# Multiplying only the used blocks in the merge levels of a chunk inverse (hybrid decoder layer, one core)

## The chip, the cores and the metric

The kernel runs on one core of a Trainium2 chip. The metric is the device time of one execution in microseconds (us), taken as the median of three runs. Lower is better.

## What is computed

The reference is one step of a one-layer hybrid decoder: a short convolution group and a gated delta network (GDN) group of 4 heads side by side, then a feed-forward layer. All of it is float32. This change touches one place only, the triangular solve inside a chunk of the GDN:

```python
lower = jnp.where(strict, jnp.einsum('nbhid,nbhjd->nbhij', kb, kc) * decay, 0.0)
eye = jnp.eye(chunk, dtype=jnp.float32)
...
sol = lax.linalg.triangular_solve(eye + lower, rhs, left_side=True, lower=True)
```

The kernel works with chunks ("tiles") of 128 tokens, so for each of the 8 prompt tiles t = 1 to 8 and each of the 4 heads it needs the inverse of a 128x128 unit lower triangular matrix.

## The kernel before

Everything is placed by hand in one instruction stream for each engine, with semaphores between them.

**Stages.** First the input projection (`w_in`, 28 weight tiles n, each multiplied in three column groups g, so the projection runs in units u = 3n + g). Then the output projection, the up projection and the down projection. A projection product is written as three float32r products (high x high, low x high, high x low: `dense_part`, L1699 to L1701). TensorE goes through these without a break. The GDN's small products are laid between the units by an order written out by hand: from unit u = 42 on, `round_step(u)` gives the tile t and a step s from 1 to 5, and `round_part(t, s)` issues that step right behind the dense part of its unit, on TensorE and on VectorE alike.

**The inverse.** The 32x32 blocks on the diagonal are inverted earlier. They are loaded as `X` (the inverse so far) and `Y` (its transpose), [128, 4 x 128], heads side by side. `At` is the transpose of the lower matrix. Two merge levels, k = 5 (blocks of 32 to 64) and k = 6 (64 to 128), each do: `level_p` multiplies `At` with `X` (L1919), VectorE's `keep_p` writes the product into `pairs{k}` (`pb[k]`) times a 0/1 mask that keeps only the blocks wanted (L2694), `level_xy` multiplies that with `Y` in both orders (level 5: L1932 and L1933, level 6: only L1933), and `keep_xy` subtracts the results from `X` (L2702, level 5 only) and `Y` (L2704). All results go through one PSUM bank, `L_BANK`.

**The steps of a round** for tile t, with a = t - 1, on TensorE: s = 1 `use_state(a)` (L1950, L1954), then `level_p(t, 5)`; s = 2 `next_state(a)` (L1964, L1967), then `level_xy(t, 5)`; s = 3 `level_p(t, 6)`, then `turn_k` (transposes, L1885); s = 4 `turn_o(a)` (transposes, L1977), `level_xy(t, 6)`, then `products_qk` (L1879); s = 5 `state_of_k` (L1902, it waits for level 6's `xy_kept`) and `turn_v`. Between two steps lies one unit of dense work. In the first round (t = 1) there is no tile a before it in this form. There `sample_states` (L2042, products with 48 rows) stands in front of each of the four steps.

**How a matmul shows.** A plain float32 matmul leaves two records on TensorE (and two weight loads). So the 4 heads of one level product are 8 records. A float32r product leaves one. A form such as `48*128 48x512` is read: 48 rows of the array (the contraction) by 128 columns (the stationary operand's), and a moving operand of 48 partitions x 512 elements.

**Masks and zeros.** The masks for the levels are a constant table, loaded to `c_levels` (`cg`, L730) by SyncE's queue. GpSimd zeroes `pairs5` and `pairs6` once (L1011, semaphore `pb_zero`), since `keep_p` writes only half of the columns. `pairs6` as zeros also feeds the DMAs that clear scratch memory (L734 to L737).

Of the kernel before, what the change touches and what calls it, by code (L numbers as in the profile page):

```python
# [7 lines left out]
ALU = mybir.AluOpType  # L8
# [5 lines left out]
P = 128  # L14
# [3 lines left out]
NH = 4  # L18
# [18 lines left out]
LEVELS = (5, 6)  # L37

# [39 lines left out]
NG = NH * (NT - 1)  # L78


def constants():
# [15 lines left out]
    g = []  # L97
    for k in LEVELS:
        b = 2 ** k
        first = np.arange(P // 2) // b  # L100
        r = np.arange(P)
        g.append(((r[:, None] // (2 * b) == first[None, :]) & (r[:, None] % (2 * b) >= b)).astype(np.float32))
# [4 lines left out]
    g.append(ahead)  # L107
    return main, np.concatenate(g, axis=1).astype(np.float32)


def build(nc, x_prompt, x_sample, state_conv_a, state_conv_qkv, state_ssm, meta_tokens, norm_mix, w_in,
# [4 lines left out]
    with ctx:  # L116
# [120 lines left out]
        cg = place("c_levels", [P, P], F32, FREE + 7 * HB)  # L237
        ahead_big = place("ahead_big", [P, P], F32, FREE + 7 * HB + 512)
        assert FREE + 7 * HB + 1024 <= R1
        lev = {k: cg[:, P // 2 * i:P // 2 * (i + 1)] for i, k in enumerate(LEVELS)}  # L240

# [124 lines left out]
        s_levels = sem("s_levels"); s_ahead = sem("s_ahead"); s_states = sem("s_states")  # L366
# [226 lines left out]
        def first(ap, b):  # L593

            return ap.rearrange("p (n two b) -> p n two b", two=2, b=b)[:, :, 0, :]

        def second(ap, b):
            return ap.rearrange("p (n two b) -> p n two b", two=2, b=b)[:, :, 1, :]

        def per_head(ap, c, w):  # L600

            return ap.unsqueeze(2).to_broadcast([c, NH, w])

# [51 lines left out]
        def _(sp):  # L655
# [69 lines left out]
            def step(u):  # L725
                n, g = u // 3, u % 3
                if g == 0 and n == 1:
                    sp.wait_ge(x_turned, 3 * KT)
                    sp.dma_start(g_picks[:, :], c_main[0:2 * NG, 2 * P + 2 * C0 + 2 * NH:]).then_inc(s_ahead, 16)
                    sp.dma_start(cg[:, :], c_gdn[:, 0:P]).then_inc(s_levels, 16)  # L730
                    sp.dma_start(ahead_big[:, :], c_gdn[:, P:2 * P]).then_inc(s_ahead, 16)
                    sp.dma_start(ahead_small[:, :], c_gdn[:, 2 * P:2 * P + C0]).then_inc(s_ahead, 16)
                    sp.wait_ge(pb_zero, 2)
# [209 lines left out]
        def _(pool):  # L943
# [62 lines left out]
            def zero_pairs():  # L1006

                pool.wait_ge(ab_made, 3)
                pool.wait_ge(rows_kept, 3)
                for k in LEVELS:  # L1010
                    pool.memset(pb[k][:, :], 0.0).then_inc(pb_zero, 1)  # L1011
# [680 lines left out]
        def _(pe):  # L1692
# [212 lines left out]
            def level_p(t, k):  # L1905
# [11 lines left out]
                for h in range(NH):  # L1917
                    hs = slice(P * h, P * h + P)
                    ins = pe.matmul(ps[L_BANK][:, hs], At[:, hs], X[:, hs], start=True, stop=True)  # L1919
                ins.then_inc(p_made, 1)  # L1920

            def level_xy(t, k):
# [6 lines left out]
                for h in range(NH):  # L1929
                    hs = slice(P * h, P * h + P)  # L1930
                    if not last:
                        pe.matmul(ps[L_BANK][:, hs], Y[t % 2][:, hs], pb[k][:, hs], start=True, stop=False)  # L1932
                    ins = pe.matmul(ps[L_BANK][:, hs], pb[k][:, hs], Y[t % 2][:, hs], start=last, stop=True)  # L1933
# [399 lines left out]
        def _(dve):  # L2333
# [351 lines left out]
            def keep_p(t, k):  # L2685
                m, b = len(LEVELS) * (t - 1) + LEVELS.index(k), 2 ** k
                dve.wait_ge(p_made, m + 1)
                if t == 1:
                    dve.wait_ge(s_levels, 16)
                    dve.wait_ge(zeroed, 16 * (2 * NT - 1))  # L2690
                src = ps[L_BANK][:, :].rearrange("p (h n two b) -> p h n two b", h=NH, two=2, b=b)[:, :, :, 0, :]
                dst = pb[k][:, :].rearrange("p (h n two b) -> p h n two b", h=NH, two=2, b=b)[:, :, :, 0, :]
                mask = lev[k].rearrange("p (n b) -> p n b", b=b).unsqueeze(1).to_broadcast([P, NH, P // 2 // b, b])
                dve.tensor_tensor(dst, src, mask, ALU.mult).then_inc(p_kept, 1)  # L2694
# [614 lines left out]
```

## Time and profile before

| | us |
|---|---|
| median of 3 runs | 1294.07 (1293.22 to 1294.09) |
| the profiled execution's own time | 1292.4 |
| its span in the profile | 1290.6 |
| TensorE matmul busy in the span | 1271.4 (99%) |
| VectorE busy | 811.9 (63%) |
| GpSimd busy | 658.5 (51%) |
| ScalarE busy | 462.2 (36%) |

The span is the time between the first and the last instruction that the profiler recorded. The profiled execution is 1.8 us longer than its span, and 1.7 us under the median. Busy times of matmuls are modelled and overlap each other, so the price of a matmul in a stream is read from the distance between the starts of two records, not from how long one record is. The granted TensorE clock is 0.997 of full speed over the span.

### The profile page before, as it was taken

The page shows a single profiled execution, that of the slowest core. Times are in us where ns is not written, and L with a number is a line of the kernel's source. Part 1 is how long each engine was busy: PE and PEld are TensorE (multiplying, and loading weights), DVE is VectorE, ACT ScalarE, POOL GpSimd, SP SyncE. Part 2 cuts the span into 40 slices and gives each one's busy share as a digit, 9 for nine tenths or more (in the row PEclk, how much of TensorE's full clock was granted, in tenths as well). Part 3 has the DMA queues.
Part 4 walks back from the last instruction along what each step waited for, and adds up shares of the span by engine and source line. Part 5 has one row for each costly group of instructions (what it writes and reads, how often), then busy time and mean ns, then how long its engine had stood idle before and what let it go on. Part 6 is the DMA issues. An engine that isn't in the chain of part 4 may idle for free.

```text
span 1290.6 us, 23252 instructions
## 1 busy us (share of the span) xinstructions
PE 1271.4 (99%) x9392; PEld 1240.8 (96%) x9392; DVE 811.9 (63%) x1252; ACT 462.2 (36%) x769; POOL 658.5 (51%) x501
## 2 busy tenths in 40 slices
PE   7999999999999999999999999999999999999997
PEld 6899999899999999999989999999999999999997
DVE  6566799434555647655887775656567767557446
ACT  7566562122212212323423233332444533333303
POOL 1322112111212111212689988888879989788701
PEclk9999999999999999999999999999999999999999
DMA  6222561743332222222134434434655343542002
GB/s 199 59 80 79 161 193 52 189 134 95 88 82 68 80 74 76 86 80 67 34 135 174 150 143 150 155 121 167 219 188 201 140 160 102 181 137 85 17 18 118
DMA packets 164860, 152.91 MB, mean 118 GB/s; under 512 B 21111, under 2 KB 141459, under 8 KB 162066
## 3 DMA queue, kind: packets, MB, share of 16 engines
q1 hardware_dynamic: 141778, 138.55, 33.3%
q10 hardware_dynamic: 22976, 12.88, 3.7%
q8 instruction: 75, 1.23, 0.4%
q14 instruction: 31, 0.25, 0.1%
HBM read 104.11 MB, written 47.29 MB: 117 GB/s over the span
## 4 chain that ended last, share of the span: by engine, by line
PE 89%; DVE 4%; issue 3%; ACT 1%; POOL 1%; DMA 1%; SPq 0%; POOLq 0%; DVEq 0%; ACTq 0%
PE banks L2224 15%; PE banks L2227 15%; PE banks L2226 15%; PE banks L1699 10%; PE banks L1701 10%; PE banks L1700 10%; PE banks L2271 1%; PE banks L2272 1%; PE banks L2273 1%; PE banks L1919 1%; PE banks L1933 1%; PE banks L2155 1%; DMA w_raw<-in_w_in 1%; DVE hT L3119 1%; PE banks L2279 1%
## 5 line engine op out<-in xcount | busy, mean ns | idle before, releaser
L1699 PE MATMUL banks<-xn_high,w_high 128*128 128x384 f32 (+1 forms) x672 | 227.5, 338 | 1.2 <-DVE xn_low L2369 1.2
L1701 PE MATMUL banks<-xn_high,w_low 128*128 128x384 f32 (+1 forms) x672 | 218.7, 325 | 0.0
L1700 PE MATMUL banks<-xn_low,w_high 128*128 128x384 f32 (+1 forms) x672 | 218.5, 325 | 0.0
L959 POOL TENSOR_TENSOR w_low<-w_raw,w_high 128x1024 fp32r<-128x1024 f32 x30 | 75.0, 2500 | 232.8 <-ACT w_high L1219 232.8
L2224 PE MATMUL banks<-op_high,set_high 128*128 128x264 f32 x672 | 191.3, 285 | 0.2
L2227 PE MATMUL banks<-op_high,set_low 128*128 128x264 f32 x672 | 190.8, 284 | 0.0
L2226 PE MATMUL banks<-op_low,set_high 128*128 128x264 f32 x672 | 190.5, 283 | 0.0
L3119 DVE TENSOR_TENSOR hT<-hT,banks 128x528 f32<-128x528 f32 x148 | 100.7, 700 | 106.6 <-PE banks L2227 106.2
L1102 POOL TENSOR_TENSOR set_low<-w_up_raw,set_high 128x512 fp32r<-128x512 f32 x79 | 122.7, 1553 | 60.2 <-ACT set_high L1528 60.2
L2224 PE MATMUL banks<-up_high_T,set_high 128*128 128x264 f32 x496 | 141.6, 285 | 0.9 <-POOL up_low_T L1109 0.6
L2227 PE MATMUL banks<-up_high_T,set_low 128*128 128x264 f32 x496 | 140.8, 284 | 0.0
L2226 PE MATMUL banks<-up_low_T,set_high 128*128 128x264 f32 x496 | 140.6, 283 | 0.0
L1699 PEld LDWEIGHTS banks<-xn_high,w_high 128*128 128x128 f32 x672 | 126.9, 189 | 3.9 <-DVE w_low L2363 1.2
L1700 PEld LDWEIGHTS banks<-xn_low,w_high 128*128 128x128 f32 x672 | 127.3, 189 | 0.0
L2224 PEld LDWEIGHTS banks<-op_high,set_high 128*128 128x128 f32 x672 | 126.3, 188 | 0.6 <-DVE op_low L3129 0.3
L1701 PEld LDWEIGHTS banks<-xn_high,w_low 128*128 128x128 f32 x672 | 126.7, 189 | 0.0
L2227 PEld LDWEIGHTS banks<-op_high,set_low 128*128 128x128 f32 x672 | 126.4, 188 | 0.0
L2226 PEld LDWEIGHTS banks<-op_low,set_high 128*128 128x128 f32 x672 | 126.3, 188 | 0.0
L2224 PE MATMUL banks<-up_high_B,set_high 128*128 128x264 f32 x408 | 116.5, 286 | 1.9 <-DVE u_rows L3028 1.6
L2227 PE MATMUL banks<-up_high_B,set_low 128*128 128x264 f32 x408 | 115.9, 284 | 0.0
L2226 PE MATMUL banks<-up_low_B,set_high 128*128 128x264 f32 x408 | 115.7, 284 | 0.0
L2224 PEld LDWEIGHTS banks<-up_high_T,set_high 128*128 128x128 f32 x496 | 93.2, 188 | 1.5 <-POOL up_low_T L1109 0.8
(383 smaller groups left out, 3141.7 us busy)
## 6 DMA issues: line engine op xcount, KB each, us to landing
op_raw<-ops_kept SPq DMA_DIRECT2D x21, 1056.0 KB, 5.0
w_up_raw<-in_w_up SPq DMA_DIRECT2D x16, 1024.0 KB, 5.5
ops_kept<-u_rows SPq DMA_DIRECT2D x28, 528.0 KB, 2.8
w_raw<-in_w_in SPq DMA_DIRECT2D x28, 512.0 KB, 4.1
ops_kept<-u_T SPq DMA_DIRECT2D x42, 264.0 KB, 2.0
w_down_half<-in_w_down SPq DMA_DIRECT2D x3, 2048.0 KB, 8.3
w_down<-in_w_down SPq DMA_DIRECT2D x24, 256.0 KB, 4.0
w_raw<-in_w_out SPq DMA_DIRECT2D x8, 512.0 KB, 4.0
```

The costliest lines, as they stand in the source:

```text
L959: pool.tensor_tensor(w_l[n % 2][:, :, :], w_raw[n % 2][:, :, :], w_h[n % 2][:, :, :].bitcast(F32), ALU.subtract).then_inc(w_low, 1)
L1102: pool.tensor_tensor(set_l[s % 4][:, :, :], up_source_at(s), set_h[s % 4][:, :, :].bitcast(F32), ALU.subtract).then_inc(w_low, 1)
L1699: pe.matmul(bank[:, 0:w], w_h[n % 2][:, k, :], hi[:, c0:c0 + w], start=(k == first), stop=False)
L1700: pe.matmul(bank[:, 0:w], w_h[n % 2][:, k, :], lo[:, c0:c0 + w], start=False, stop=False)
L1701: ins = pe.matmul(bank[:, 0:w], w_l[n % 2][:, k, :], hi[:, c0:c0 + w], start=False, stop=(k == last))
L1919: ins = pe.matmul(ps[L_BANK][:, hs], At[:, hs], X[:, hs], start=True, stop=True)
L1933: ins = pe.matmul(ps[L_BANK][:, hs], pb[k][:, hs], Y[t % 2][:, hs], start=last, stop=True)
L2155: ins = pe.transpose(ps[6 + m % 2][:, o:o + c], (xs0, xs)[f % 2][0:c, t, :], eye[0:c, 0:c])
L2224: pe.matmul(bank, high[:, j, :], op_high[:, j, cols], start=(j == 0 and not begun), stop=False, skip_group_check=True)
L2226: pe.matmul(bank, high[:, j, :], op_low[:, j, cols], start=False, stop=False, skip_group_check=True)
L2227: ins = pe.matmul(bank, low[:, j, :], op_high[:, j, cols], start=False, stop=(j == n - 1), skip_group_check=True)
L3119: dve.tensor_tensor(hc, hc, both, ALU.add if sign > 0 else ALU.subtract).then_inc(acc_read_dve, 1)
```

## The change

Both levels multiply only the blocks that the merge uses, as separate small matmuls, each on the part of TensorE's array that the partitions of its operands and its result select. `corner(ap, n, rows_at, cols_at)` is a 32x32 block per head of pair n (n = 0, 1) of 64 rows.

- Level 5, `level_p`: instead of one 128x128 product a head, two of 32 x 32 x 32 (n = 0 and 1). `level_xy`: instead of two 128x128 products a head, four of 32 x 32 x 32.
- Level 6, `level_p` and `level_xy`: instead of one 128x128 product a head, one of 64 x 64 x 64.
- `keep_p`: instead of one multiply with the mask (128 partitions x 256 elements), plain copies: at level 5 two of 32 partitions x 128 elements, at level 6 one of 64 partitions x 256 elements.
- `keep_xy`: at level 5 four subtractions of 32 partitions x 128 elements instead of two of 128 x 256; at level 6 one of 64 partitions x 256 elements instead of one of 128 x 256.
- The mask table, its DMA and semaphore `s_levels`, and the zeroing of `pairs5` go.

```diff
@@ constants and loads
-        cg = place("c_levels", [P, P], F32, FREE + 7 * HB)
...
-                    sp.dma_start(cg[:, :], c_gdn[:, 0:P]).then_inc(s_levels, 16)
...
-                    sp.wait_ge(pb_zero, 2)
+                    sp.wait_ge(pb_zero, 1)
...
-                for k in LEVELS:
-                    pool.memset(pb[k][:, :], 0.0).then_inc(pb_zero, 1)
+                pool.memset(pb[LEVELS[-1]][:, :], 0.0).then_inc(pb_zero, 1)
...
+        def corner(ap, n, rows_at, cols_at):
+
+            return h3(ap)[2 * B * n + rows_at:2 * B * n + rows_at + B, :, 2 * B * n + cols_at:2 * B * n + cols_at + B]
@@ level_p
-                    hs = slice(P * h, P * h + P)
-                    ins = pe.matmul(ps[L_BANK][:, hs], At[:, hs], X[:, hs], start=True, stop=True)
+                    if k == LEVELS[-1]:
+                        up, low = slice(P * h, P * h + W), slice(P * h + W, P * h + P)
+                        ins = pe.matmul(ps[L_BANK][W:P, up], At[0:W, low], X[0:W, up], start=True, stop=True)
+                    else:
+                        for n in range(2):
+                            ins = pe.matmul(corner(ps[L_BANK], n, B, 0)[:, h, :], corner(At[:, :], n, 0, B)[:, h, :],
+                                            corner(X[:, :], n, 0, 0)[:, h, :], start=True, stop=True)
@@ level_xy
-                    if not last:
-                        pe.matmul(ps[L_BANK][:, hs], Y[t % 2][:, hs], pb[k][:, hs], start=True, stop=False)
-                    ins = pe.matmul(ps[L_BANK][:, hs], pb[k][:, hs], Y[t % 2][:, hs], start=last, stop=True)
+                    if last:
+                        up, low = slice(P * h, P * h + W), slice(P * h + W, P * h + P)
+                        ins = pe.matmul(ps[L_BANK][0:W, low], pb[k][W:P, up], Y[t % 2][W:P, low], start=True, stop=True)
+                    else:
+                        for n in range(2):
+                            made = corner(pb[k][:, :], n, B, 0)[:, h, :]
+                            turned = corner(Y[t % 2][:, :], n, B, B)[:, h, :]
+                            pe.matmul(corner(ps[L_BANK], n, B, 0)[:, h, :], turned, made, start=True, stop=True)
+                            ins = pe.matmul(corner(ps[L_BANK], n, 0, B)[:, h, :], made, turned, start=True, stop=True)
@@ keep_p
-                dve.tensor_tensor(dst, src, mask, ALU.mult).then_inc(p_kept, 1)
+                if k == LEVELS[-1]:
+                    ins = dve.tensor_copy(h3(pb[k][W:P, :])[:, :, 0:W], h3(ps[L_BANK][W:P, :])[:, :, 0:W])
+                else:
+                    if t == 1:
+                        dve.wait_ge(zeroed, 16 * (2 * NT - 1))
+                    for n in range(2):
+                        ins = dve.tensor_copy(corner(pb[k][:, :], n, B, 0), corner(ps[L_BANK], n, B, 0))
+                ins.then_inc(p_kept, 1)
@@ keep_xy
-                ys = second(Y[t % 2][:, :], b)
-                dve.tensor_tensor(ys, ys, second(made, b), ALU.subtract).then_inc(xy_kept, 1)
+                if k == LEVELS[-1]:
+                    ys = h3(Y[t % 2][0:W, :])[:, :, W:P]
+                    ins = dve.tensor_tensor(ys, ys, h3(ps[L_BANK][0:W, :])[:, :, W:P], ALU.subtract)
+                else:
+                    for n in range(2):
+                        xs_, ys = corner(X[:, :], n, B, 0), corner(Y[t % 2][:, :], n, 0, B)
+                        dve.tensor_tensor(xs_, xs_, corner(ps[L_BANK], n, B, 0), ALU.subtract)
+                        ins = dve.tensor_tensor(ys, ys, corner(ps[L_BANK], n, 0, B), ALU.subtract)
+                ins.then_inc(xy_kept, 1)
```

Here `P` is 128, `W` is 64 and `B` is 32.

## Rows read from the trace of the kernel before

**Rows 1.** The page: busy times, and the chain that ended last.

```profile
PE 1271.4 (99%) x9392; PEld 1240.8 (96%) x9392; DVE 811.9 (63%) x1252; ACT 462.2 (36%) x769; POOL 658.5 (51%) x501
...
PE 89%; DVE 4%; issue 3%; ACT 1%; POOL 1%; DMA 1%; SPq 0%; POOLq 0%; DVEq 0%; ACTq 0%
```

**Rows 2.** All waits of TensorE, 240 to 500 us: total, times, longest.

```profile
PE banks L1977 <- DVE o_tok L2746: 0.2, 1, 0.2
```

**Rows 3.** Groups by line, TensorE, 240 to 500 us: busy us, mean ns.

```profile
L1933 PE MATMUL banks<-Y,pairs 128*128 128x128 f32 x128 | 20.9, 276 | 0.0
L1919 PE MATMUL banks<-X,At 128*128 128x128 f32 x128 | 17.1, 276 | 0.0
L1932 PE MATMUL banks<-pairs,Y 128*128 128x128 f32 x64 | 12.5, 277 | 0.0
```

**Rows 4.** Timeline, TensorE, steps 1 and 2 of round 2: start, us, what.

```profile
281.97 1.06 PE L1919 MATMUL banks<-X,At 128*128 128x128 f32 x8
282.79 0.39 PE L1699 MATMUL banks<-xn_high,w_high 128*128 128x304 f32 x1
...
288.00 0.39 PE L1932 MATMUL banks<-pairs,Y 128*128 128x128 f32 x2
...
289.56 0.39 PE L1933 MATMUL banks<-Y,pairs 128*128 128x128 f32 x2
289.71 0.42 PE L1699 MATMUL banks<-xn_high,w_high 128*128 128x384 f32 x1
289.97 0.34 PE L1700 MATMUL banks<-xn_low,w_high 128*128 128x384 f32 x1
```

**Rows 5.** Timeline, TensorE, steps 3 and 4 of round 2.

```profile
293.98 1.05 PE L1919 MATMUL banks<-X,At 128*128 128x128 f32 x8
294.87 0.60 PE L1885 MATMUL banks<-c_main,k_feat 128*128 128x128 f32 x4
...
299.94 1.06 PE L1933 MATMUL banks<-Y,pairs 128*128 128x128 f32 x8
300.83 0.61 PE L1879 MATMUL banks<-q_feat,k_feat 128*128 128x128 f32 x4
```

**Rows 6.** Timeline, TensorE, 245.5 to 246.2 us, step 1 of round 1.

```profile
245.02 1.02 PE L2042 MATMUL banks<-v_masked,kd_t 48*128 48x512 f32 x2
245.97 0.49 PE L1919 MATMUL banks<-X,At 128*128 128x128 f32 x2
```

**Rows 7.** Timeline, TensorE, around 178.8 us: window up to 178.86, then 179.9.

```profile
178.57 0.27 PE L1885 MATMUL banks<-c_main,k_feat 128*48 128x128 f32 x1
178.78 0.29 PE L1879 MATMUL banks<-q_feat,k_feat 128*48 128x48 f32 x2
...
178.78 0.56 PE L1879 MATMUL banks<-q_feat,k_feat 128*48 128x48 f32 x8
179.26 0.44 PE L1699 MATMUL banks<-xn_high,w_high 128*128 128x384 f32 x1
179.54 0.33 PE L1700 MATMUL banks<-xn_low,w_high 128*128 128x384 f32 x1
```

**Rows 8.** Timeline, TensorE, around 200 us: window up to 199.92, then 201.2.

```profile
199.75 0.42 PE L1891 MATMUL banks<-Y_t,kg 48*128 48x48 f32 x2
...
199.75 1.09 PE L1891 MATMUL banks<-Y_t,kg 48*128 48x48 f32 x8
200.77 0.41 PE L1699 MATMUL banks<-xn_high,w_high 128*128 128x304 f32 x1
```

**Rows 9.** Timeline, VectorE, 277 to 291 us.

```profile
277.42 1.13 DVE L2674 SCALAR_TENSOR_TENSOR vn<-banks,egn,vn 128x128 f32<-128x128 f32 x4 [2.40 <-ACT vn L1397]
...
283.07 0.42 DVE L2694 TENSOR_TENSOR pairs<-banks,c_levels 128x256 f32<-128x256 f32 x1 [0.20 <-PE banks L1919]
...
290.33 0.41 DVE L2704 TENSOR_TENSOR Y<-Y,banks 128x256 f32<-128x256 f32 x1
```

**Rows 10.** Windows: us, busy us of PE, PEld, DVE, ACT, POOL, granted clock, DMA share, GB/s.

```profile
238.60:242.00 3.40, 3.40 (x15) 2.97 (x14) 2.41 (x3) 1.65 (x8) 0.00 (x0) 0.51 0.16 53
```

More of the change, by code:

```diff
@@ L37 @@
 LEVELS = (5, 6)
+B = SOLVED
 IN_TILES = ([("k", h, O_QKV + NH * P + P * h) for h in range(NH)] + [("q", h, O_QKV + P * h) for h in range(NH)]
@@ L78 @@
 NG = NH * (NT - 1)
+W = P // 2
 def constants():
@@ L96, in constants @@
     main[:2 * NG, o + 2 * NH + NT - 1:] = row % NH == np.arange(NH)[None, :]
-    g = []
-    for k in LEVELS:
[L99 to L102, printed above, removed]
     ahead = np.zeros((P, P + C0), np.float32)
@@ L106, in constants @@
     ahead[:C0, P:] = np.where(same & up[:C0, :C0], 0, FAR_BELOW)
-    g.append(ahead)
-    return main, np.concatenate(g, axis=1).astype(np.float32)
+    return main, ahead
 def build(nc, x_prompt, x_sample, state_conv_a, state_conv_qkv, state_ssm, meta_tokens, norm_mix, w_in,
@@ L236, in build @@
         kd = place("kd", [P, NH * P], F32, FREE + 6 * HB)
-        cg = place("c_levels", [P, P], F32, FREE + 7 * HB)
-        ahead_big = place("ahead_big", [P, P], F32, FREE + 7 * HB + 512)
-        assert FREE + 7 * HB + 1024 <= R1
-        lev = {k: cg[:, P // 2 * i:P // 2 * (i + 1)] for i, k in enumerate(LEVELS)}
+        ahead_big = place("ahead_big", [P, P], F32, FREE + 7 * HB)
+        assert FREE + 7 * HB + 512 <= R1
         SB = SOLVED * SOLVED
@@ L591, in h3 @@
             return ap.rearrange("p (h i) -> p h i", h=NH)
[L593 to L598, printed above, removed]
         def per_head(ap, c, w):
             return ap.unsqueeze(2).to_broadcast([c, NH, w])
+        def corner(ap, n, rows_at, cols_at):
+            return h3(ap)[2 * B * n + rows_at:2 * B * n + rows_at + B, :, 2 * B * n + cols_at:2 * B * n + cols_at + B]
         def hrow(f):
@@ L1009, in zero_pairs @@
                 pool.wait_ge(rows_kept, 3)
-                for k in LEVELS:
-                    pool.memset(pb[k][:, :], 0.0).then_inc(pb_zero, 1)
+                pool.memset(pb[LEVELS[-1]][:, :], 0.0).then_inc(pb_zero, 1)
             def identities():
@@ L2685, in keep_p @@
             def keep_p(t, k):
-                m, b = len(LEVELS) * (t - 1) + LEVELS.index(k), 2 ** k
+                m = len(LEVELS) * (t - 1) + LEVELS.index(k)
                 dve.wait_ge(p_made, m + 1)
[L2688 to L2693, printed above, removed]
-                dve.tensor_tensor(dst, src, mask, ALU.mult).then_inc(p_kept, 1)
+                if k == LEVELS[-1]:
[6 more added lines that the diff above has]
+                ins.then_inc(p_kept, 1)
             def keep_xy(t, k):
-                m, b = len(LEVELS) * (t - 1) + LEVELS.index(k), 2 ** k
+                m = len(LEVELS) * (t - 1) + LEVELS.index(k)
                 dve.wait_ge(xy_made, m + 1)
-                made = ps[L_BANK][:, :]
-                if k != LEVELS[-1]:
-                    xf = first(X[:, :], b)
-                    dve.tensor_tensor(xf, xf, first(made, b), ALU.subtract)
-                ys = second(Y[t % 2][:, :], b)
-                dve.tensor_tensor(ys, ys, second(made, b), ALU.subtract).then_inc(xy_kept, 1)
+                if k == LEVELS[-1]:
[7 more added lines that the diff above has]
+                ins.then_inc(xy_kept, 1)
             def keep_v(t):
```

7 lines of the change are left out of this document (3 added, 4 removed).

## The prediction

> **What bounds the kernel.** I read the page first, for who is busy and who is last: TensorE's matmuls fill 99% of the span and 89% of the chain that ended last [rows 1]. Then the waits, to see whether TensorE ever stands for something else in the stretch that changes: in 240 to 500 us it waits 0.2 us in all [rows 2]. So whatever TensorE saves there shortens the kernel, and whatever it pays there lengthens it. The work that the change touches is 128 + 64 + 128 = 320 records [rows 3]. Their mean of 276 ns is a pipelined length, not a price. The price is the pitch between starts: the timeline of one round has 8 records between 293.98 and 294.87 and again between 299.94 and 300.83 [rows 5], 0.112 us each. All 320 cost 35.7 us of TensorE.
>
> **Prices for small blocks.** No row shows a 32x32 or 64x64 block, so I take them from the narrowest forms, and read four numbers from two groups of 8 records. I write m for the columns of the stationary operand and n for those of the moving one.
>
> - Pitch in the stream: with m = n = 48, records 3 to 8 add 0.56 - 0.29 = 0.27 us, or 0.045 each [rows 7]. With m = 128, n = 48 they add 1.09 - 0.42 = 0.67, or 0.112 [rows 8], the same as 128x128. So the larger of m and n sets it, and a line through both is 0.005 us + 0.00084 per column: 0.0315 at 32, 0.0585 at 64.
> - Entering: the first narrow record starts 178.78 - 178.57 = 0.21 us behind the last full one [rows 7] where 0.11 is usual, so going from the whole array to a part costs about 0.09.
> - The second record of a group is not overlapped: its distance is a group of two less the length of its last record (0.208 for 48x48, 0.27 for the others): 0.29 - 0.21 = 0.08 at 48x48 [rows 7], 0.42 - 0.27 = 0.15 at 128 and 48 [rows 8], 0.49 - 0.28 = 0.21 at 128 and 128 [rows 6]. That is load and multiply one behind the other, 0.053 at 32 and 0.107 at 64.
> - Leaving: the last narrow record starts at 178.78 + 0.56 - 0.21 = 179.13, the dense work at 179.26, 0.13 to 0.14 later; from the group with m = 128 it is 200.77 - (199.75 + 1.09 - 0.27) = 0.20 [rows 8]. So leaving is the pitch plus 0.09: 0.12 at 32, 0.15 at 64. The dense record after that follows at 0.28 [rows 7], where it is 0.26 in an ordinary exit [rows 4].
>
> **TensorE, step by step, t = 2 to 8.** Each stretch runs from the last untouched record before the level product to the second one after it.
>
> - Step 1: before, 0.11 in, 8 x 0.112 to the dense work less the overlap of its start, which is 282.79 - 281.97 = 0.82 [rows 4], then 0.26: 0.11 + 0.82 + 0.26 = 1.19. After, 16 records: 0.20 + 0.053 + 14 x 0.0315 + 0.12 + 0.28 = 1.09. Saved 0.10.
> - Step 2: before, 0.11 + (289.97 - 288.00) = 2.08 [rows 4]. After, 32 records: 0.20 + 0.053 + 30 x 0.0315 + 0.12 + 0.28 = 1.60. Saved 0.48.
> - Step 3: before, 0.17 in, 0.89 for the records [rows 5], 0.11 to the second transpose: 1.17. After, 8 records at 64: 0.27 + 0.107 + 6 x 0.0585 + 0.15 + 0.14 (the usual 0.11 and some of the lost overlap) = 1.02. Saved 0.15.
> - Step 4: before, 0.11 + 0.89 [rows 5] + 0.11 = 1.11. After: 0.20 + 0.107 + 0.351 + 0.15 + 0.21 (two full loads in a row, [rows 6]) = 1.02. Saved 0.09.
>
> That is 0.82 us a tile, 5.7 us for seven. In the first round the level products stand behind `sample_states`, which uses 48 rows: the kernel before pays there already, 0.52 where 0.43 is usual and 0.21 where 0.11 is [rows 6]. So entering is 0.19 cheaper in each of the four steps, and the tile saves 0.82 + 0.76 = 1.6 us. Sum: 7.3 us. Note how little level 6 and step 1 bring: about 60% of the arithmetic's saving is given back at the eight changes between whole array and part in each round. Step 2 alone carries 60% of the gain, and only if 32-wide records really come every 0.03 us.
>
> **VectorE and the waits.** At level 5 `keep_p` becomes two operations of 128 elements for one of 256, `keep_xy` four for two. A 128-element operation that reads PSUM costs 1.13 / 4 = 0.28 us, one with 256 costs 0.41 to 0.42 [rows 9]. So VectorE pays 6 x 0.28 - 3 x 0.42 = +0.44 us a tile, 3.5 us in all. Level 6 keeps its 256 elements a partition, and I cost it at nothing. None of this is on the path: the level 5 product is kept at 283.5 [rows 9] and used at 288.00 [rows 4], `keep_xy` ends at 290.7 [rows 9] and step 3 needs it at 293.98 [rows 5]. The cover is 3.2 us against +0.3 us. Queued behind `keep_xy` in step 3 is `keep_k`, whose reader is two dense units away. If the cover were gone, the cost would be that 0.3 us a tile, 2.4 us. The mask's DMA (SyncE's queue, with two small loads behind it) and one memset of GpSimd go at 41 to 47 us, where TensorE waits for neither queue: nothing.
>
> **Sum.** Against the profiled execution: span 1290.6 - 7.3 = 1283.3, its time 1292.4 - 7.3 = 1285.1. The median of the runs lies 1.7 above that execution, so 1294.07 - 7.3 = 1286.8 us.
>
> **Rivals.**
>
> - *Parts run side by side: faster still.* At level 5 neighbouring matmuls alternate between parts of the array (n = 0 and 1; in step 2 also two column parts): 7 changes of part in step 1 and 15 in step 2. If each change cost only 0.005 us of a pitch, it would save 0.027 x 22 = 0.6 us a tile, 4.8 in all: 1282.0. Against it: the pitch at m = 128, n = 48 is set by the weight load [rows 8], and loads would have to overlap too. The Trainium skill (TensorEngine Tiling (Array Packing), Key Properties) says that they do: different tiles execute weight loads and matmuls in parallel. No row of this trace has two parts at work, so it can't agree or disagree; by that rule the time is this rival's. Chance 0.15.
> - *Small records don't come faster than 0.045 us.* The narrowest stream here is 0.045 [rows 7], and a floor of issue could sit just there. Then level 5 costs 48 x 0.0135 = 0.65 us a tile more, 5.2 in all: a gain of 2.1, 1292.0, no change. Between that row and the line's 0.0315 I take the line, since rows 7 and 8 show the price following the columns. Chance 0.13.
> - *A change of part drains the array: slower.* Going from whole to part costs 0.09 and the lost overlap of the next record 0.02. If going from one part to another of the same size costs the same, 0.11, then if only changes of row part count, 14 a tile x 0.11 = 1.5 us, 12 us in all and 1299; if all 22 count, 19 us and 1306. It decides at 0.91 / 22 = 0.04 us a change, which is 0.065 with 14. The Trainium skill (TensorEngine Tiling (Array Packing), Gotcha 1) speaks for it: different row tiles cannot access the same PSUM bank simultaneously, and all these results go to one bank. Its Key Properties speak against it, for they name a drain only where the mode changes, not the tile. If only the overlap of load and multiply is lost at a change (0.0215 each), the gain is 3.5 us, still faster. Chance of slower 0.13.
> - *The clock falls.* Behind a long row of 48-wide products the granted clock was 0.51 for 3.4 us [rows 10], some 1.7 us lost. That is the lower level, 1.2 GHz. Once behind each step 2, it would cost 13.6 us: 1300. Against: each level stretch here is 1.0 to 1.6 us, with dense work before and behind. Chance 0.04.
> - *Something that TensorE didn't wait for is late* (VectorE's extra time, a weight tile): 1292, chance 0.03.
>
> **Chances and range.** The forecast, a gain between 3.5 (overlap lost at each change) and 9.8 (0.025 us a record at level 5), 1284.3 to 1290.6, has 0.52. About 0.2% (2.6 us) is what a measurement of this kernel tells from no change. Faster: 0.52 + 0.15 and a third of the floor rival, as a floor of 0.04 still gives 4 us: 0.71. Same: 0.12. Slower: 0.13 + 0.04: 0.17. The range reaches down to the overlap rival and up past the floor rival, leaving out the drain and the clock: 1281.0 to 1294.5.
>
> **What the changed profile would show.** 512 records in place of 320. Step 1's 16 records from first to last start in 0.50 us and step 2's 32 in 1.0 if the pitch is right; 0.7 and 1.4 with the floor; about 1.3 and 1.8 with a drain at changes of row part. Each level group entered 0.20 us behind the record before, left by its pitch plus 0.09. In the first round no extra at the entry. TensorE's waits in 240 to 490 us still near zero and clock 1.00. VectorE with 24 more operations (8 a tile for 5) and 3.5 us more. I am wrong if the pitch at level 5 isn't 0.03, if entering from a transposing matmul to 64 columns costs more than the 0.09 seen at 48, or if the time saved comes back as TensorE waits in the projections behind.

## The result, and the profile after

The changed kernel takes 1280.13 us (median of 4 runs, 1279.20 to 1281.01), the kernel before 1293.64 us on the same chip (1291.47 to 1294.09). The ratio is 0.9896 (95% interval 0.9884 to 0.9908): 13.5 us faster. The forecast was 1286.8, with a range whose lower end was 1281.0. The sign was right and the gain 6.2 us too small. The remaining 0.4 us is the lower median of the kernel before in this comparison. The profiled execution took 1279.97 us, its span is 1278.2.

The page of the kernel after, busy times and then the chain that ended last, beside [rows 1]:

```profile
PE 1257.5 (98%) x9584; PEld 1221.3 (96%) x9584; DVE 821.8 (64%) x1276; ACT 462.4 (36%) x769; POOL 656.3 (51%) x500
...
PE 90%; DVE 5%; issue 3%; ACT 1%; DMA 1%; SPq 0%; POOLq 0%; POOL 0%; DVEq 0%; ACTq 0%
```

TensorE is still the bound. It has 192 records more, and 14 us less of busy time. Groups by line and form, TensorE, 240 to 500 us of the kernel after, to be read beside [rows 3] (busy us, mean ns of one):

```profile
L1908 PE MATMUL banks<-X,At 64*64 64x64 f32 x64 | 5.4, 224 | 0.0
L1925 PE MATMUL banks<-Y,pairs 64*64 64x64 f32 x64 | 5.4, 224 | 0.0
L1931 PE MATMUL banks<-Y,pairs 32*32 32x32 f32 x128 | 3.6, 194 | 0.0
L1930 PE MATMUL banks<-pairs,Y 32*32 32x32 f32 x128 | 3.6, 194 | 0.0
L1911 PE MATMUL banks<-X,At 32*32 32x32 f32 x128 | 3.5, 194 | 0.0
```

All 320 records of [rows 3] have become 512. The mean of one fell only from 276 to 194 ns, and again it is not the price. At level 5 a record is 194 ns long, yet 128 of them fill 3.5 us of busy time, 0.027 us each. Busy time here is the union of overlapping records, and so many are in flight at once.

Timeline of the kernel after, TensorE, step 1 of round 2, then the first records and the exit of step 2 (start, us, what), beside [rows 4]:

```profile
279.64 0.44 PE L1911 MATMUL banks<-X,At 32*32 32x32 f32 x16
280.01 0.41 PE L1687 MATMUL banks<-xn_high,w_high 128*128 128x304 f32 x1
...
285.34 0.21 PE L1930 MATMUL banks<-pairs,Y 32*32 32x32 f32 x1
285.35 0.21 PE L1931 MATMUL banks<-Y,pairs 32*32 32x32 f32 x1
285.35 0.21 PE L1930 MATMUL banks<-pairs,Y 32*32 32x32 f32 x1
285.36 0.21 PE L1931 MATMUL banks<-Y,pairs 32*32 32x32 f32 x1
285.39 0.19 PE L1930 MATMUL banks<-pairs,Y 32*32 32x32 f32 x1
...
285.60 0.19 PE L1931 MATMUL banks<-Y,pairs 32*32 32x32 f32 x1
285.72 0.45 PE L1687 MATMUL banks<-xn_high,w_high 128*128 128x384 f32 x1
```

Step 1's group of 16 starts at 279.64 and ends at 280.08; less the 0.19 of its last record, its records start within 0.25 us. I had predicted 0.50. In step 2 the 32 records start between 285.34 and 285.60, in 0.26 us, where I had predicted 1.0. The four parts (n = 0 and 1, each with a product of either order) start 6 or 7 ns apart. The next record of the same part comes some 0.03 us behind the last (0.05 for a part's second record). So the price that I put on every record, 0.0315, is the price of a record on its own part, and four parts pay it at the same time. Step 2 has four times the arithmetic of one part and takes no longer than step 1, which uses two.

Steps 3 and 4 of the same round, beside [rows 5]:

```profile
289.84 0.34 PE L1689 MATMUL banks<-xn_high,w_low 128*128 128x384 f32 x1
290.11 0.67 PE L1908 MATMUL banks<-X,At 64*64 64x64 f32 x8
290.71 0.55 PE L1873 MATMUL banks<-c_main,k_feat 128*128 128x128 f32 x3
...
295.73 0.27 PE L1975 MATMUL banks<-c_main,o_tok 128*128 128x128 f32 x1
295.93 0.68 PE L1925 MATMUL banks<-Y,pairs 64*64 64x64 f32 x8
296.54 0.49 PE L1867 MATMUL banks<-q_feat,k_feat 128*128 128x128 f32 x2
```

Here everything is as priced: entered 0.27 behind a dense record and 0.20 behind a transpose, and 0.60 and 0.61 us from the first narrow record to the work behind (0.107 + 6 x 0.0585 + 0.15 = 0.61). The 64x64 products all use one part.

The waits of TensorE, 240 to 500 us (total, times, longest), beside [rows 2]:

```profile
PE banks L1975 <- DVE o_tok L2748: 0.7, 2, 0.4
PE banks L1687 <- DVE ya_low L2577: 0.5, 1, 0.5
```

1.2 us in place of 0.2, but only the first line is new. The wait for `ya_low` is there in the kernel before too, just behind the window of [rows 2]:

```profile
507.45 0.40 PE L1699 MATMUL banks<-ya_high,w_high 128*128 128x288 f32 x1 [0.48 <-DVE ya_low L2579]
```

With everything some 14 us earlier, it has moved into the window. So the waits for `o_tok` rose from 0.2 to 0.7 us, and that is all. On VectorE the level's operations in the same window are these (busy us, mean ns):

```profile
L2692 DVE COPY pairs<-banks 32x128 f32<-32x128 f32 x16 | 4.6, 290 | 0.4
L2704 DVE TENSOR_TENSOR X<-X,banks 32x128 f32<-32x128 f32 x16 | 4.6, 287 | 0.4
L2705 DVE TENSOR_TENSOR Y<-Y,banks 32x128 f32<-32x128 f32 x16 | 4.5, 280 | 0.2
L2687 DVE COPY pairs<-banks 64x256 f32<-64x256 f32 x8 | 3.4, 427 | 4.7 <-PE banks L1908 4.5
L2700 DVE TENSOR_TENSOR Y<-Y,banks 64x256 f32<-64x256 f32 x8 | 3.2, 401 | 0.0
```

That is 20.3 us. Before, the level's operations took 16.6 there, so VectorE does 3.7 us more (3.5 predicted).

**Where the 13.5 us come from.** I aligned the two traces on the same dense records. Between 211 us of the kernel before and 518 us, the end of the last round, the kernel after gains 16.0 us. Of this 15.2 are the levels: that much shorter are the stretches of the four steps (from the last untouched record to the second one behind), added up over the eight tiles, 13.0 at level 5 and 2.2 at level 6. It is also what the 7.3 of my sum and 0.98 us a tile x 8 = 7.9 at level 5 make together. Another 1.5 is the clock fall of [rows 10], which this execution doesn't show. About 0.7 goes back to the waits for `o_tok`: there the transposes start 0.72 and 0.58 us behind the record before them, in rounds 3 and 4, where the kernel before has 0.18 and 0.45. The span is only 12.4 shorter, though. 1.65 us are lost at the start, where the full clock was first granted at 17.7 us instead of 13.4, and 1.9 us behind this line of VectorE's timeline in the kernel after:

```profile
636.09 8.27 DVE L3081 SCALAR_TENSOR_TENSOR u_rows<-u_rows,h_squares 128x1056 f32<-128x1056 f32 x1
644.28 0.69 DVE L3052 TENSOR_TENSOR u_rows<-u_rows,banks 128x528 f32<-128x528 f32 x1
```

The same operation took 2.06 us in the kernel before. TensorE waited 3.2 us for its successor (1.6 in the kernel before), and the granted clock fell behind the wait for 3.4 us. The first experiment asks whether that belongs to the change.

### The profile page after: what moved, and what is told of

Read it like the earlier page. It is cut to its first block, busy times and chain, and to the rows that moved or that the text cites. A ratio compares the mean times of both kernels' runs of the same rounds, so it can differ in the third digit from the quotient of the medians.

```text
span 1278.2 us, 23657 instructions
## 1 busy us (share of the span) xinstructions
PE 1257.5 (98%) x9584; PEld 1221.3 (96%) x9584; DVE 821.8 (64%) x1276; ACT 462.4 (36%) x769; POOL 656.3 (51%) x500
## 4 chain that ended last, share of the span: by engine, by line
PE 90%; DVE 5%; issue 3%; ACT 1%; DMA 1%; SPq 0%; POOLq 0%; POOL 0%; DVEq 0%; ACTq 0%
PE banks L2222 15%; PE banks L2225 15%; PE banks L2224 15%; PE banks L1687 10%; PE banks L1689 10%; PE banks L1688 10%; PE banks L2269 1%; PE banks L2270 1%; PE banks L2271 1%; PE banks L2153 1%; PE banks L1867 1%; DMA w_raw<-in_w_in 1%; DVE hT L3121 1%; PE banks L2277 1%; PE banks L2040 1%
```

## The experiments

Theories. **A**: parts of the array run side by side, so a level 5 step costs what its busiest part costs. **B**: the small records are simply cheaper than I thought, one behind another, each some 0.016 us in step 1 and 0.008 in step 2. Other candidates are VectorE's new form, the missing mask and its DMA, and chance events outside the rounds. The expectations of by_part and level6_columns use the letters A and B for pairs of their own, which they spell out.

| kernel | median us (range, runs) | before us | ratio (95%) |
|---|---|---|---|
| copy | 1279.35 (1278.89 to 1282.68, 6) | 1293.29 | 0.9905 (0.9890 to 0.9920) |
| level6_only | 1291.28 (1289.56 to 1293.68, 12) | 1293.29 | 0.9986 (0.9977 to 0.9996) |
| level5_only | 1283.44 (1280.72 to 1283.62, 6) | 1293.29 | 0.9923 (0.9910 to 0.9936) |
| by_part | 1282.74 (1281.44 to 1287.40, 6) | 1293.29 | 0.9930 (0.9912 to 0.9948) |
| one_pair | 1280.31 (1278.04 to 1281.16, 4) | 1293.83 | 0.9895 (0.9880 to 0.9910) |
| twice | 1284.45 (1282.20 to 1285.44, 5) | 1293.83 | 0.9921 (0.9908 to 0.9933) |
| vector_only | 1293.25 (1291.56 to 1295.77, 11) | 1293.83 | 0.9995 (0.9987 to 1.0004) |
| same_size_together | 1277.14 (1274.95 to 1277.87, 4) | 1293.83 | 0.9866 (0.9852 to 0.9879) |
| by_two | 1278.88 (1277.03 to 1281.71, 5) | 1295.43 | 0.9888 (0.9869 to 0.9907) |
| level6_columns | 1276.35 (1274.19 to 1277.39, 4) | 1295.43 | 0.9861 (0.9838 to 0.9884) |

**copy.** The changed kernel once more, with no edit.

> The changed kernel once more. If its time is its own, about 1280 us again, 13.5 under the kernel before. In its profile: the level 5 records again 6 ns apart on different parts, 16 records of step 1 from first to last start in 0.25 us and 32 of step 2 in 0.26. Open is whether three things of its first profile come again: full clock granted 4.3 us later at the start (1.65 us lost), one VectorE operation of 8.3 us at 636 us (normally 1.2), and the fall of the clock behind TensorE's wait for it at 645 us. If they are chance, they are gone or elsewhere.

1279.35 us. In its profile the same operation of VectorE is ordinary, and there is no clock fall at 645 us:

```profile
636.74 2.07 DVE L3081 SCALAR_TENSOR_TENSOR u_rows<-u_rows,h_squares 128x1056 f32<-128x1056 f32 x1
```

So the 8.27 us were an event of one execution. GpSimd's timelines beside it, first in the kernel after, then in the copy, show what went with it:

```profile
636.99 1.29 POOL L1090 TENSOR_TENSOR set_low<-w_up_raw,set_high 128x512 fp32r<-128x512 f32 x1
...
641.98 1.26 POOL L1090 TENSOR_TENSOR set_low<-w_up_raw,set_high 128x512 fp32r<-128x512 f32 x1
```

```profile
637.61 2.35 POOL L1090 TENSOR_TENSOR set_low<-w_up_raw,set_high 128x512 fp32r<-128x512 f32 x1
```

In the kernel after, GpSimd's operations follow each other without a gap up to 643.24, each 1.3 us long, and VectorE's operation ends only behind them, at 644.36. In the copy VectorE's operation is short, and GpSimd's, started during it, is the one that takes 1.1 us more. So one of the two engines stood while the other worked, and in the first profile it was VectorE, through five operations of GpSimd. That is read from these two profiles and was not tested.

From first to last start the levels' groups agree with those of the first profile to 0.01 us in every round. The ledger is now simpler: start of the kernel -2.1 us (full clock granted at 18.5 us), 211 to 518 us +15.8, everything behind 0. The waits for `o_tok` are there again, 0.8 us in all, so these do belong to the change. The longer one is in step 4 of round 3, where `turn_o` waits while VectorE still works through the convolution taps ahead of it (one of these takes 2.36 us at 319.05, where 0.23 is usual, beside an operation of GpSimd; the kernel before has such a stretch of 2.2 us in the same round):

```profile
325.19 0.55 PE L1975 MATMUL banks<-c_main,o_tok 128*128 128x128 f32 x3 [0.51 <-DVE o_tok L2748]
```

From round 2 to round 3 the level 5 product comes 1.78 us sooner than before (28.61 us apart instead of 30.39). My step prices with side by side parts give 0.82 + 0.98 = 1.80. The next round brings only 1.02. The wait of 0.5 us falls in it, and with the wait the overlap of the records around it is lost: the transposes start 0.85 us behind the record before them, where 0.18 is usual.

**level6_only and level5_only.** Each keeps one level's products as before (128x128) and has the other's as after. VectorE is as after in both. `level_xy` is edited like `level_p`, and level6_only zeroes `pairs5` as before, since its 128x128 products read all of it.

```diff
# level6_only, in level_p and level_xy, level 5
-                        for n in range(2):
-                            ins = pe.matmul(corner(ps[L_BANK], n, B, 0)[:, h, :], corner(At[:, :], n, 0, B)[:, h, :],
-                                            corner(X[:, :], n, 0, 0)[:, h, :], start=True, stop=True)
+                        hs = slice(P * h, P * h + P)
+                        ins = pe.matmul(ps[L_BANK][:, hs], At[:, hs], X[:, hs], start=True, stop=True)
# level5_only, level 6
-                        ins = pe.matmul(ps[L_BANK][W:P, up], At[0:W, low], X[0:W, up], start=True, stop=True)
+                        hs = slice(P * h, P * h + P)
+                        ins = pe.matmul(ps[L_BANK][:, hs], At[:, hs], X[:, hs], start=True, stop=True)
```

> Level 6's 64x64 products alone, level 5's matmuls 128x128 as before (its corners copied by VectorE, pairs5 zeroed again). Both theories price it at 0.24 us a tile plus 0.38 in the first round, 2.3 us: about 1291.3. If entering and leaving the 64x64 part cost more than the 0.09 us each that I took, it is no gain at all, 1293.6.

> Level 5 as in the changed kernel, level 6's matmuls again 128x128 (VectorE's operations as in the changed kernel). Theory, parts work side by side at level 5: level 6 is worth 0.24 us a tile and 0.38 more in the first round, 2.3 us, so this keeps 11.2 of the 13.5 us: about 1282.4. Rival, level 5's records come one behind the other as I priced them and the gain beyond the forecast is from elsewhere: 7.3 - 2.3 = 5.0 us under before, 1288.6.

level6_only gained 2.0 us (0.5 to 3.0), 2.2 by the stretches of its steps 3 and 4: the 64x64 prices were right. level5_only gained 9.9 us, with an interval of 8.3 to 11.6. With level 5 at my prices it would have gained about 5. So the surprise sits in level 5 alone. In the profile of level5_only the stretches of steps 1 and 2 are 13.0 us shorter than before, just as in the changed kernel. From 211 us to the end of the rounds it gains 12.3, the rest going to the waits for `o_tok`. Its start loses 1.95 us and a clock fall at 59 us another 1.55, so its span is 8.8 shorter. Losses of this kind are most likely why the medians give less than the stretches.

**by_part.** The level 5 products of one part stand together, and then those of the next part. Same records, other order.

```diff
-                for h in range(NH):
...
-                        for n in range(2):
+                    for n in range(2):
+                        for h in range(NH):
                             ins = pe.matmul(corner(ps[L_BANK], n, B, 0)[:, h, :], corner(At[:, :], n, 0, B)[:, h, :],
...
                             pe.matmul(corner(ps[L_BANK], n, B, 0)[:, h, :], turned, made, start=True, stop=True)
+                        for h in range(NH):
+                            made = corner(pb[k][:, :], n, B, 0)[:, h, :]
+                            turned = corner(Y[t % 2][:, :], n, B, B)[:, h, :]
                             ins = pe.matmul(corner(ps[L_BANK], n, 0, B)[:, h, :], made, turned, start=True, stop=True)
```

> Same matmuls as the changed kernel, but at level 5 all four heads of one part are issued before the next part begins, so that neighbours in the stream are on the same part. Theory A, parts only overlap when neighbours in the stream are on different parts: step 1 takes 0.50 us and step 2 1.0 again, 0.98 us a tile more, 7.9 in all: about 1288. Theory B, the engine looks past matmuls that wait for their part to later ones on a free part: no change, 1280, and the records of different parts stand 6 ns apart, out of the program's order.

Neither number came. The order does matter: step 1 took 0.40 us and step 2 0.70, where it was 0.25 and 0.26. That makes 0.59 us a tile and 4.7 us in all by the trace, and 3.4 by the medians, of runs that spread over 6 us; in part the later TensorE waits less for `o_tok` (0.3 us for 0.8). Theory B, in which a record's price doesn't depend on its neighbour, falls with this. But the parts still overlap in part. Timeline of by_part, step 2 of round 2:

```profile
289.41 0.34 PE L1932 MATMUL banks<-pairs,Y 32*32 32x32 f32 x5
289.56 0.21 PE L1936 MATMUL banks<-Y,pairs 32*32 32x32 f32 x1
289.59 0.19 PE L1932 MATMUL banks<-pairs,Y 32*32 32x32 f32 x1
...
289.98 0.32 PE L1936 MATMUL banks<-Y,pairs 32*32 32x32 f32 x5
290.23 0.45 PE L1687 MATMUL banks<-xn_high,w_high 128*128 128x384 f32 x1
```

Five records of the first part start alone; then a record of the second part starts right behind the fifth, and the two alternate. The second part's records stand behind all 8 of the first part's in the program. So the first part's sixth, seventh and eighth records were already out of the way when the second part's first one began, and it started ahead of them. The account that fits is a queue in front of each part. Records leave in program order, each part can hold three waiting records behind the one at work, and a fourth stops the stream for everybody. Starts of the four parts by that account: 0, 0.148, 0.306, 0.459, last record at 0.70. Measured: 0, 0.153, 0.306, 0.460 and 0.702. It was formed after this run and from it, so it needed another.

**by_two.** The four heads in two pairs, and inside each pair the order of by_part.

```diff
-                for h in range(NH):
...
-                        for n in range(2):
+                    for h2 in (0, 2):
+                      for n in range(2):
+                        for h in (h2, h2 + 1):
```

> As by_part, but only two heads (4 records) of one part stand together before the next part begins. In the trace of by_part the second part's first record started 6 ns behind the fifth of the first part's eight, so with three records still waiting between them. If the engine can pass over three waiting records, then here the second part begins at once and two parts are always at work: step 1 takes 0.25 to 0.28 us from first to last start (0.40 in by_part), step 2 about 0.50 (0.70 in by_part, 0.26 in the changed kernel), 0.26 us a tile more than the changed kernel, 2.1 us: about 1281.5. If it can't look ahead at all, step 1 takes 0.45 and step 2 0.9: 1286.

Step 1 took 0.269 us, as expected. Step 2 took 0.295 to 0.297, not 0.50. (This profile lists a granted clock of 0.95 up to 1150 us, but its rounds keep the copy's pace to 0.5%, 28.75 us from round 2 to 3 for 28.61, so the steps can be set beside the others.) Its first records are these:

```profile
286.77 0.21 PE L1934 MATMUL banks<-pairs,Y 32*32 32x32 f32 x1
286.79 0.21 PE L1938 MATMUL banks<-Y,pairs 32*32 32x32 f32 x1
286.80 0.21 PE L1934 MATMUL banks<-pairs,Y 32*32 32x32 f32 x1
286.81 0.21 PE L1938 MATMUL banks<-Y,pairs 32*32 32x32 f32 x1
```

All four parts are at work within 0.04 us, though the fourth part's first record stands behind 12 others in the program, 9 of which had not started. So a limit of three records for all parts together, on which I had built the 0.50, is wrong. With three waiting places for each part, no part of by_two ever has a fourth one in wait at the start, and the stream runs freely. That limit fits both kernels. It rests on the starts in these two, and a test made for it alone was not run. At 1278.88 us this kernel can't be told from the copy.

**one_pair.** It leaves out the second block pair (n = 1) of level 5, on TensorE and VectorE, so that half of level 5's products and of its operations on VectorE are not done.

```diff
-                        for n in range(2):
+                        for n in range(1):
```

> Leaves work out: at level 5 only the first pair of blocks (n = 0) is multiplied and kept, so half of level 5's matmuls and of its VectorE operations are gone and the lower half of the inverse isn't merged at this level. Theory, parts work side by side and a part takes 0.032 us a record: the first part's 8 records in step 1 and the 8 on each of two parts in step 2 still take 0.25 us each, so the time is that of the changed kernel, 1279.4 us within 0.5. Rival, the engine simply issues small records every 0.016 and 0.008 us whichever part they are on: step 1 and step 2 shrink to half, 0.25 us a tile, 2 us less: 1277.4.

The timeline of step 1, round 2, of one_pair, 8 records where the changed kernel has 16:

```profile
280.30 0.43 PE L1911 MATMUL banks<-X,At 32*32 32x32 f32 x8
280.67 0.41 PE L1687 MATMUL banks<-xn_high,w_high 128*128 128x304 f32 x1
```

0.37 us from the first record to the dense work, as with 16 records (279.64 to 280.01). First to last it is 0.243 for 0.249, and in step 2 0.250 for 0.263. Half of the multiplying left out saves TensorE 0.02 us a tile, and the time, 1280.31, is that of the changed kernel. This is the plainest evidence for theory A: the second row part is free.

**twice.** Each level 5 product is issued twice, into the same place.

```diff
-                        for n in range(2):
+                        for n in (0, 1, 0, 1):
```

> At level 5 each product is made twice over (same result), so every part has 16 records instead of 8 in both steps; neighbours in the stream are still on different parts. Theory: a part takes 0.032 us a record, so both steps go from 0.25 to 0.51 us between first and last start, 0.51 us a tile more, 4.1 us: about 1283.4. If the issue of records were the limit in step 2 (64 records, 0.006 apart would be 0.38), step 2 would stay under 0.51.

In step 1 of round 2 it is 0.62 us from the first record (282.31) to the dense work (282.93), 0.503 of them first to last; step 2's 64 records took 0.562. A step costs 8 records of its part more, 0.25 to 0.30. Step 2 went past the 0.51 that I expected: its first 32 records start within 0.263 us, as in the changed kernel, but the other 32 need 0.288, where 8 records of a part at 0.0315 make 0.25. So issue at 6 ns a record was not the limit, but with four parts and 64 records something slows the stream a little, and no run shows what. With eight tiles that is 4.4 us by the trace, and the medians differ by 5.1 (1284.45 and 1279.35, of two comparisons).

**vector_only.** The kernel before on TensorE, with VectorE's copies and corner subtractions, no masks and no mask DMA. `pairs5` is zeroed as before.

```diff
-                dve.tensor_tensor(dst, src, mask, ALU.mult).then_inc(p_kept, 1)
+                    for n in range(2):
+                        ins = dve.tensor_copy(corner(pb[k][:, :], n, B, 0), corner(ps[L_BANK], n, B, 0))
```

> TensorE's level products are the 128x128 ones of the kernel before, only VectorE's part of the change is in: unmasked copies of the corners, 64 operations for 40, 3.5 us more of VectorE by my working; pairs5 zeroed as before. It was costed at nothing: 1293.3 within 0.5. If VectorE's extra time were on the path somewhere, up to 3 us more: 1296.

A ratio of 0.9995: nothing, as priced. The masks, their load and 3.7 us of VectorE are worth nothing either way while TensorE comes no earlier.

**same_size_together.** The changed kernel, with the 48-row products of tile 0 regrouped (`use_state` and `next_state` of tile 0), so that matmuls of one form follow each other. Two small ones elsewhere are swapped for the same reason.

```diff
                 for h in range(NH):
-                    hs, cs = slice(P * h, P * h + P), slice(C0 * h, C0 * h + C0)
+                    hs = slice(P * h, P * h + P)
                     pe.matmul(ps[S_BANK][:, hs], kd0[:, hs], v_meta[:, hs], start=True, stop=True)
+                for h in range(NH):
+                    hs, cs = slice(P * h, P * h + P), slice(C0 * h, C0 * h + C0)
                     ins = pe.matmul(ps[O_BANK][0:C0, hs], qk0[:, cs], vnew[0:C0, hs], start=True, stop=True)
```

> The changed kernel, and in addition the products of tile 0 that alternate between 48 and 128 rows or columns are put together by size: in next_state0 four of L2029's kind and then four of L2030's, in use_state0 the same (only the first product of the bank opens with the flag that clears it), and two products of the decay sums are swapped. If every change of size costs 0.09 us and the lost overlap of the record behind it (0.035 to 0.10), 6 changes less in next_state0 save 1.0 us, 6 in use_state0 0.75, 2 in the sums 0.2: 1.9 us in all, 1277.4. If the price stems from the level products' own place only, nothing: 1279.4.

Timeline of the copy, first and last row of `next_state` of tile 0:

```profile
238.12 0.49 PE L2027 MATMUL banks<-v_meta,kd_t 48*128 48x128 f32 x2
...
240.82 0.42 PE L2028 MATMUL banks<-v_new,qk 48*48 48x128 f32 x2
241.16 0.41 PE L1687 MATMUL banks<-xn_high,w_high 128*128 128x304 f32 x1
```

The same in same_size_together:

```profile
236.52 1.16 PE L2031 MATMUL banks<-v_meta,kd_t 48*128 48x128 f32 x8
237.60 1.07 PE L2034 MATMUL banks<-v_new,qk 48*48 48x128 f32 x8
238.60 0.41 PE L1687 MATMUL banks<-xn_high,w_high 128*128 128x304 f32 x1
```

3.04 us became 2.08. In `use_state` of tile 0 it is 0.78 less. 12 changes between forms go, 6 in each, so one costs 0.13 to 0.16 us. Of these 1.7 us the profile gives 0.4 back in round 3, where the level 5 product starts 0.57 us behind the record before it instead of 0.21; the profile names no releaser. The kernel takes 1277.14 us, 2.2 less than the copy of another comparison; against the kernel before the two ratios are 0.9866 and 0.9905. I had expected 1.9.

**level6_columns.** same_size_together, with each 64x64 product of level 6 cut into two of 64 rows x 32 columns, on two column parts.

```diff
-                        ins = pe.matmul(ps[L_BANK][W:P, up], At[0:W, low], X[0:W, up], start=True, stop=True)
+                        for c in range(2):
+                            o = W + B * c
+                            ins = pe.matmul(ps[L_BANK][o:o + B, up], At[0:W, P * h + o:P * h + o + B], X[0:W, up],
+                                            start=True, stop=True)
```

> same_size_together, and in addition each 64x64x64 product of level 6 is made as two products with 32 columns of the stationary operand each (64 rows, moving operand 64 columns), on two column parts. Theory A, the larger of the stationary and the moving columns sets a part's pitch: 0.058 us a record still, both parts side by side, so 16 records take 0.46 us from first to last start as 8 did: 1277.1, no change. Theory B, the columns of the weight load set it: 0.032, 0.25 us instead of 0.46 in two steps, 3.3 us less: 1273.8.

```profile
288.43 0.64 PE L1910 MATMUL banks<-X,At 64*32 64x64 f32 x16
289.00 0.55 PE L1873 MATMUL banks<-c_main,k_feat 128*128 128x128 f32 x3
```

0.42 us from the first to the last of 16 records, against 0.457 for 8 undivided ones. The 64 moving columns still set the pitch (0.056), and halving the stationary columns saves mostly at a part's second record (0.080 for 0.107). The two steps save 0.07 us a tile, 0.56 in all; 1276.35 against 1277.14 is no difference that these runs can tell. It is still the fastest kernel of the study by its median, with same_size_together beside it.

## Why the prediction was wrong

**The step that failed** is the price of level 5's records in the stream. In steps 1 and 2 I wrote "14 x 0.0315" and "30 x 0.0315", one record behind another. The line through [rows 7, 8] was right for one part: in one_pair 8 records on one row part took 0.243 us, where 0.053 + 6 x 0.0315 gives 0.242. What was wrong is that the records add up over parts. Step 1 cost 0.25 instead of 0.49 and step 2 0.26 instead of 1.00: 0.98 us a tile, 7.9 in all. That is the whole miss of 6.2 us in the gain and 1.7 us more. The waits for `o_tok` give back 0.7 to 0.9 of it; the rest is within the interval of the comparison (1.5 us either way).

**The rival "parts run side by side"** was the right one, and I mis-sized it twice. It got 0.15, and its price was wrong. I let only the change from one part to the next be cheap ("only 0.005 us of a pitch"), so that a pair of records still cost 0.0365; that gave 4.8 us more. But records that run side by side are not a chain with cheap links. The cost is the longest part's own records, 8 in both steps, and so step 2 costs what step 1 costs. That form of the sentence gives 7.9 us, and 1278.9 as the time, before the new waits. The measured step times of 0.249 and 0.262 differ only by the 6 or 7 ns of the other parts' starts. The Trainium skill (TensorEngine Tiling (Array Packing), Key Properties) says that different tiles can execute weight loads and matmuls in parallel. The trace agrees, with four parts started 6 to 7 ns apart; one_pair shows that a second row part costs 0.02 us a tile, and twice that 8 more records on each part cost 0.25 to 0.30 us a step.

**The drain rival** is refuted: neighbouring records on different row parts, with results in the same PSUM bank, start 6 or 7 ns apart, where it wanted 0.11 us. It had leaned on the sentence of the Trainium skill (TensorEngine Tiling (Array Packing), Gotcha 1) that different row tiles cannot access the same PSUM bank simultaneously. Here products on two row parts (0 and 2 in step 1, 1 and 3 in step 2) write different partitions of one bank, and none waits for it; the measurement decides.

**The floor of 0.045** is refuted too: 0.032 on one part, 0.008 over four.

**What held.** Entering at 0.20 behind a full record (205 ns measured at 32, 202 and 268 at 64). The second record's 0.107 at 64. The pitch of 0.0585 at 64 (58 to 59 ns). Leaving at 0.12 and 0.15 (120 and 149 ns). No extra at the entry in the first round. Steps 3 and 4 as a whole, which level6_only shows by itself: 1291.28. VectorE's +3.5 us (3.7), off the path as long as TensorE keeps its old pace (vector_only). The mask and its DMA at nothing (vector_only, which still has the memset of `pairs5`; no run took that out alone). The clock: 1.00 in the rounds of the changed kernel.

**What was off by little.** I had TensorE's waits stay near zero. Those for `o_tok` rose by 0.5 us, 0.7 with the overlap lost around them, since a TensorE that comes to round 3 some 6 us earlier reaches `o_tok` before VectorE has written it. vector_only, with the same VectorE work and TensorE at its old pace, waits 0.2 as before, so the added work alone doesn't open them. The pace alone doesn't either: one_pair keeps the pace and has half of VectorE's level 5 operations, fewer microseconds of them than even the kernel before, and its wait in round 3 is gone (the transposes start 0.18 us behind the record before). As far as these runs show, it takes both. So "none of this is on the path" was off by up to 0.7 us. The cover of 3.2 us that I named in step 3 was never touched. A clock fall costs 1.5 us by the alignment, where I had read 1.7 from its length.

**What stays open.** Why VectorE stood beside GpSimd's work through 8.27 us in one execution, where in the others such stretches add about 2.2 us at most. Why the second half of step 2 slows in twice. And why the start of the kernel reaches the full clock anywhere between 12.1 and 18.9 us, which moves a run by about 2 us whatever the kernel.

## What to carry to other kernels

Small matmuls on different parts of the array are not to be priced as a stream: count the records of the busiest part, at that part's own pitch, add the entry and the exit once, and interleave the parts in the program so that no part has more than a few records queued. When a product splits into blocks, first ask how many parts it can occupy at once; here the level with four parts gave 13.0 us of the 15.2, and the level with one part the rest. Put matmuls of one form behind each other, since a change of form cost about 0.15 us here, and look at what the bound engine reaches early once it has become faster.

## What the runs showed of the hardware that was not expected

- **Matmuls start out of program order.** A record whose part is free starts ahead of earlier ones that wait for theirs: 3 records passed over in by_part, 9 in by_two. What fits both is three waiting places in front of each part.
- **A part's pitch is set by the larger of its column counts, and up to 8 records on each of four parts the parts don't slow each other:** 0.032 us a record at 32x32 with one part at work or four (8 records in 0.243 and 0.249 us on one and two row parts), 0.056 for pairs of 64*32. With 16 records on each of four parts (twice) step 2 took 0.562 us where step 1, on two parts, took 0.503.
- **An operation of VectorE and one of GpSimd seem to stretch each other** (read from two profiles, not tested): 8.27 us in place of 2.07 on VectorE, or 2.35 in place of 1.29 on GpSimd, at the same place in two executions of one kernel.
- **The clock falls behind narrow products only in some executions.** The stretch at 240 us of by_part in its profile (us, busy us of PE, PEld, DVE, ACT, POOL, granted clock, DMA share, GB/s):

```profile
240.00:246.50 6.50, 6.50 (x32) 5.40 (x31) 2.41 (x3) 2.12 (x10) 0.00 (x0) 0.74 0.54 181
```

  and the stretch of the copy that starts at the same record, where it didn't fall:

```profile
238.70:245.20 6.50, 6.50 (x39) 5.02 (x38) 2.41 (x3) 2.06 (x10) 0.00 (x0) 1.00 0.56 187
```

  Both start in tile 0's narrow products and go on into the dense records behind; in the same 6.5 us one has 32 records and the other 39. Where the clock fell, here and in [rows 10], it was at 1.2 GHz for 3.4 us and cost about 1.5. The profiles have none to two such falls, which may be much of the spread between runs of one kernel.
